# Two queues in place of one: the weight loads of a fused transformer kernel issued by ScalarE, the transfers through DRAM by SyncE

## The reference

```
first stack, per layer:
    z = rmsnorm(x) @ w_in            -> four kinds of attention, 4 heads each:
        block attention (rope), forget-gate attention, latent attention (up-projections), dilated mixture
    x += rmsnorm(concat(heads) @ w_out)
    x += rmsnorm((silu(h @ w_gate) * (h @ w_up)) @ w_down),   h = rmsnorm(x),  d_ff = 2816
second stack, per layer:
    x += 0.5 * rmsnorm(swiglu(rmsnorm(x)))                    d_ff = 2816
    b, c, v, p, gates = rmsnorm(x) @ w_in_2                   (width 6 * 1024)
    y = g_a * ((b * conv3(c * v)) @ w_conv_out) + g_p * (pool_mixer(p) @ w_pool_out)
    x += rmsnorm(y @ w_o)
    x += 0.5 * rmsnorm(swiglu(rmsnorm(x)))
```

## Time and profile before

| | us |
|---|---|
| three runs, median (lowest to highest) | 1735.21 (1733.9 to 1736.9) |
| the profiled execution, its own time | 1734.06 |
| its span, first to last instruction | 1732.3 |
| PE busy | 1720.9 (99%) |
| PEld busy | 1427.8 (82%) |
| DVE busy | 1232.8 (71%) |
| ACT busy | 924.6 (53%) |
| POOL busy | 117.6 (7%) |

### The profile page before, as it was taken

How to read it: one execution, slowest core, us unless ns; L and a number is a source line. 1 busy time by engine, 2 the same in 40 slices (tenths; PEclk the granted TensorE clock), 3 DMA queues, 4 the chain that set the end, 5 groups by cost and what they waited for, 6 DMA issues and landing times.

```text
span 1732.3 us, 22131 instructions
## 1 busy us (share of the span) xinstructions
PE 1720.9 (99%) x8077; PEld 1427.8 (82%) x8077; DVE 1232.8 (71%) x1581; ACT 924.6 (53%) x1438; POOL 117.6 (7%) x263
## 2 busy tenths in 40 slices
PE   9999999999999999999999999999999999999998
PEld 7888888888888888888888888888888888878887
DVE  8986656898655766666986866676656697686665
ACT  7665445767444554455564544465445556455443
POOL 5300000321000100000000100000000100010000
PEclk9999999999999999999999999999999999999999
DMA  8658776676777688768775777768786877568773
GB/s 269 196 179 255 231 231 196 189 227 209 234 230 227 215 242 255 236 206 278 231 254 204 223 242 230 228 213 254 243 253 198 268 236 251 205 201 256 232 221 122
DMA packets 351580, 392.84 MB, mean 227 GB/s; under 512 B 90512, under 2 KB 280496, under 8 KB 351216
## 3 DMA queue, kind: packets, MB, share of 16 engines
q1 hardware_dynamic: 348992, 383.68, 70.4%
q0 software_dynamic: 2176, 7.75, 1.4%
q10 hardware_dynamic: 304, 0.01, 0.0%
HBM read 357.82 MB, written 33.55 MB: 226 GB/s over the span
## 4 chain that ended last, share of the span: by engine, by line
PE 95%; DVE 2%; DMA 1%; POOL 1%; issue 0%; ACT 0%; DVEq 0%; SPq 0%; POOLq 0%; ACTq 0%
PE Dp L2407 28%; PE Gp L2407 19%; PE Tp L2407 19%; PE Dp L2375 8%; PE Dp L2376 8%; PE Dp L2377 8%; PE Dp L2427 2%; PE Gp L2615 1%; DVE wlo L1586 1%; PE Tp L2390 0%; DMA Z<-held_piece 0%; PE Dp L2646 0%; PE Tp L2646 0%; DMA stage<-held_piece 0%; DMA held_piece<-dil_masks 0%
## 5 line engine op out<-in xcount | busy, mean ns | idle before, releaser
L1586 DVE TENSOR_TENSOR wlo<-raw,whi 128x1024 fp32r<-128x1024 f32 (+1 forms) x608 | 716.9, 1215 | 259.5 <-ACT whi L1067 258.9
L1067 ACT ACTIVATE whi<-raw 128x1024 fp32r<-128x1024 f32 (+1 forms) x608 | 607.0, 1045 | 349.7 <-PE Dp L2407 96.4
L2407 PE MATMUL Dp<-whi,a_hi 128*128 128x512 f32 (+1 forms) x668 | 179.6, 390 | 0.4 <-DVE a_lo L1658 0.3
L2407 PE MATMUL Dp<-whi,a_lo 128*128 128x512 f32 (+1 forms) x668 | 178.0, 387 | 0.0
L2407 PE MATMUL Dp<-wlo,a_hi 128*128 128x512 f32 (+1 forms) x668 | 177.2, 387 | 0.0
L2407 PEld LDWEIGHTS Dp<-wlo,a_hi 128*128 128x128 f32 x668 | 124.8, 188 | 25.5 <-DVE wlo L1586 0.4
L2407 PEld LDWEIGHTS Dp<-whi,a_lo 128*128 128x128 f32 x668 | 124.6, 188 | 25.1
L2407 PEld LDWEIGHTS Dp<-whi,a_hi 128*128 128x128 f32 x668 | 122.7, 188 | 26.3 <-DVE a_lo L1658 1.5
L2375 PE MATMUL Dp<-whi,b_hi 128*128 128x512 f32 (+1 forms) x364 | 144.4, 397 | 0.0
L2377 PE MATMUL Dp<-whi,b_lo 128*128 128x512 f32 (+1 forms) x364 | 141.4, 389 | 0.0
L2376 PE MATMUL Dp<-wlo,b_hi 128*128 128x512 f32 (+1 forms) x364 | 141.4, 389 | 0.0
(11 more groups left out here) (298 smaller groups left out, 2223.8 us busy)
## 6 DMA issues: line engine op xcount, KB each, us to landing
raw<-in_ffn_w_gate_up SPq DMA_DIRECT2D x176, 512.0 KB, 5.0
raw<-in_w_in SPq DMA_DIRECT2D x132, 512.0 KB, 4.9
raw<-in_ffn_w_down SPq DMA_DIRECT2D x88, 512.0 KB, 4.4
raw<-in_w_gate SPq DMA_DIRECT2D x44, 512.0 KB, 4.0
raw<-in_w_up SPq DMA_DIRECT2D x44, 512.0 KB, 5.1
raw<-in_w_down SPq DMA_DIRECT2D x44, 512.0 KB, 4.4
held<-Z SPq DMA_DIRECT2D x132, 128.0 KB, 4.4
Z<-held SPq DMA_DIRECT2D x132, 128.0 KB, 4.7
```

The source lines that it names most:

```text
L1067: return nc.scalar.activation(whi[g % W][0:rows, c0:c0 + n], raw[g % R][0:rows, c0:c0 + n], ACT.Copy).then_inc(hi_done, 1)
L1586: return V.tensor_tensor(wlo[g % W][0:rows, c0:c0 + n], raw[g % R][0:rows, c0:c0 + n], whi[g % W][0:rows, c0:c0 + n].bitcast(F32), ALU.sub ...
L2407: return mm(bank, a[:, 4 * h + k, tile(t)], w[g % W][:, n * k:n * k + n], start=start, stop=stop, skip_group_check=True)
```

## The change

The list of what each unit loads is built ahead of all engines in a table `source`. SyncE issues units 0, 1 and 2 and from then on only what `behind(g)` issues. From unit 3 on ScalarE issues the weights: in `hi_b(g)`, so between the first and the second half of the cast of unit g, it waits for split_done of unit g-1 and issues the two DMAs of unit g+2.

```diff
-            def put(g, parts):
-                if g >= R:
-                    sp.wait_ge(split_done, 2 * (g - R) + 2)
-                if g == 0:
...
-                    return
-                for dst, src in parts:
-                    sp.dma_start(dst, src).then_inc(loaded[g % R], 16)
-                behind(g)
+            for g in range(LAST + 1):
+                first, second = source[g]
                 if g == 0:
+                    sp.dma_start(*first).then_inc(first_loaded, 16)
+                    sp.dma_start(*second).then_inc(loaded[0], 16)
                     x_half(1, 0)
                     x_half(0, 1)
                     x_half(1, 1)
+                elif g < R:
+                    sp.dma_start(*first).then_inc(loaded[g], 16)
+                    sp.dma_start(*second).then_inc(loaded[g], 16)
+                if g:
+                    behind(g)
...
+            def load(g):
+                act.wait_ge(split_done, 2 * (g - R) + 2)
+                first, second = source[g]
+                act.dma_start(*first).then_inc(loaded[g % R], 16)
+                act.dma_start(*second).then_inc(loaded[g % R], 16)
+
             def hi_b(g):
                 if g == 0:
                     act.wait_ge(loaded[0], 16)
+                elif g + R - 1 <= LAST:
+                    load(g + R - 1)
```

More of the change, by code:

```diff
@@ L583, in p_moved, with put, rows, half_rows @@
             return p_blocks[1].rearrange("p (q h e s) -> p h e q s", q=4, h=H, e=2)[:, h, e]
+        source = {}
+        def put(g, parts):
+            source[g] = parts
+        def rows(w):
+            return w.rearrange("l (k p) n -> l p k n", p=P)
+        def half_rows(g, w, l, h, c0, n):
+            r = raw[g % R][:, 0:4 * n].rearrange("p (k n) -> p k n", k=4)
+            put(g, [(r[:, 2 * e:2 * e + 2, :], w[l, :, 4 * h + 2 * e:4 * h + 2 * e + 2, c0:c0 + n])
+                    for e in range(2)])
@@ new lines, in all_rows, with two_rows, gate_up @@
+        def all_rows(g, w, l, c0):
+            r = raw[g % R][:, :].rearrange("p (k n) -> p k n", k=NK)
+            put(g, [(r[:, 4 * e:4 * e + 4, :], w[l, :, 4 * e:4 * e + 4, c0:c0 + 256]) for e in range(2)])
+        def two_rows(g, w, l, k0):
+            r = raw[g % R][:, :].rearrange("p (k n) -> p k n", k=2)
+            put(g, [(r[:, e:e + 1, :], w[l, :, k0 + e:k0 + e + 1, :]) for e in range(2)])
+        def gate_up(g, wg, wu, l, h, g0, u0):
+            r = raw[g % R][:, :].rearrange("p (k e n) -> p k e n", k=4, e=2)
+            put(g, [(r[:, :, 0, :], wg[l, :, 4 * h:4 * h + 4, g0:g0 + FC]),
+                    (r[:, :, 1, :], wu[l, :, 4 * h:4 * h + 4, u0:u0 + FC])])
@@ new lines, in build @@
+        w_in, w_out = rows(A["w_in"]), rows(A["w_out"])
+        w_g, w_u, w_d = rows(A["w_gate"]), rows(A["w_up"]), rows(A["w_down"])
+        q_up = A["w_mla_q_up"].rearrange("l (k p) n -> l p k n", p=QRH)
+        for l in range(LAYERS):
+            b = base1(l)
+            for h in range(2):
+                half_rows(b + LAT0 + h, w_in, l, h, C_LAT, LAT)
+            for h in range(2):
+                half_rows(b + MQ0 + h, w_in, l, h, C_MOBA, 512)
+            all_rows(b + MV, w_in, l, C_MOBA + 512)
+            for h in range(2):
+                half_rows(b + DQ0 + h, w_in, l, h, C_DIL, 512)
+            u = raw[(b + UPS) % R]
+            put(b + UPS, [(u[:, 0:512], A["w_mla_kv_up"][l]),
+                          (u[0:QRH, 512:1280].rearrange("p (k n) -> p k n", k=2), q_up[l])])
+            all_rows(b + DV, w_in, l, C_DIL + 512)
+            for h in range(2):
+                half_rows(b + FQ0 + h, w_in, l, h, C_FOX, 512)
+            all_rows(b + FV, w_in, l, C_FOX + 512)
+            for u, k0 in ((OUT_M, 0), (OUT_D, 6), (OUT_L, 4), (OUT_F, 2)):
+                two_rows(b + u, w_out, l, k0)
+            swiglu(b + FFN1, w_g, w_u, w_d, l, 0)
@@ new lines, in build, with project @@
+        w_in2, w_po, w_co, w_o = (rows(A[n]) for n in ("w_in_2", "w_pool_out_2", "w_conv_out_2", "w_o_2"))
+        gu1, gu2 = rows(A["ffn1_w_gate_up_2"]), rows(A["ffn2_w_gate_up_2"])
+        dn1, dn2 = rows(A["ffn1_w_down_2"]), rows(A["ffn2_w_down_2"])
+        wpg = A["w_pool_group_2"].rearrange("l g (k p) n -> l p g k n", p=P)
+        for l in range(LAYERS):
+            b = mixer2(l)
+            swiglu(base2(l), gu1, gu1, dn1, l, DFF)
+            def project(u, w, c0):
+                for c in range(2):
+                    for h in range(2):
+                        half_rows(b + u + 2 * c + h, w, l, h, c0 + 512 * c, 512)
+            project(0, w_in2, 3 * DM)
+            project(4, w_in2, DM)
+            project(8, w_in2, 2 * DM)
+            r = raw[(b + PG) % R][:, :].rearrange("p (g k n) -> p g k n", g=4, k=2)
+            put(b + PG, [(r[:, 2 * e:2 * e + 2, :, :], wpg[l, :, 2 * e:2 * e + 2, :, :]) for e in range(2)])
+            project(13, w_in2, 0)
+            project(17, w_in2, 4 * DM)
+            project(21, w_in2, 5 * DM)
+            project(25, w_po, 0)
+            project(29, w_co, 0)
+            for h in range(2):
+                for c in range(2):
+                    half_rows(b + 33 + 2 * h + c, w_o, l, h, 512 * c, 512)
+            swiglu(b + 37, gu2, gu2, dn2, l, DFF)
@@ L786, in all_rows @@
[L786 to L868, removed]
```

26 lines of the change are left out of this document (18 added, 8 removed).

## The result

| | before | after |
|---|---|---|
| time, us (median, lowest to highest) | 1734.7 (1733.9 to 1736.9) | 1749.45 (1747.49 to 1751.16) |
| ratio to before | | 1.0083 [1.0071, 1.0095] |
| span of the profiled execution, us | 1732.3 | 1747.7 |
| idle time of TensorE in it, us | 11.4 | 22.7 |

The changed kernel is 0.83% slower, 14.75 us by the medians. The forecast was slower by 4.5 us, 1739.7 us with a range up to 1747.5, so the direction came out and the size was off by a factor of three.

The account below looks back on a forecast made before the run. TensorE was taken as the bound, busy 1720.9 of 1732.3 us. Losses of 5.25 (first mixers) + 0.7 (stage ends) - 1.9 (last mixer) + 0.4 (first casts behind it) gave 4.45 us slower: 1739.7 us, range 1734.5 to 1747.5.

Parts of the forecast that it names:

- The steady state: In the FFNs, loads issued 2 us later still land in time and the pair costs zero to 0.1 us.
- Rival A: The pair is hidden behind the first half nowhere, 0.9 us more per tight cast: 11.7 us slower, 1747 us; chance 0.18.
- Places 1 and 3: First mixer at 28 to 32 us, first layer: 1.65 us lost; end of the first mixer, both layers: 1.5 us each.
- Place 2: Second layer's first mixer at 319 us: second half 1.85 us late, ScalarE's idle 0.86 us before line 1263; cost 1.0 us.
- The last mixer: End of the second layer's last mixer: the fetch flies nearly alone, so the 1.9 us wait for b_lo goes.
- Rival B: Transfers through DRAM get no faster, the 1.9 us stay, another 1.5 lost: 7.85 us slower, 1743 us; chance 0.14.
- Sum of the first mixers: Both layers' first mixers: 1.65 + 1.0 + 3.0 - 0.2 - 0.2 = 5.25 us lost.
- The lock that the forecast names: Issuing engines share a descriptor generator that each issue must lock; ScalarE's pair would at times wait, some tenths longer.
- Ends of stages: At the ten ends of stages together, 0.7 us for tenths not visible; the FFN ends were said to have slack.

Follow-up runs that it names:

- the first experiment: Changed kernel, but SyncE issues the weights cast in each layer's first mixer (units 2 to 19) in its old order: 1735.88 us, ratio 1.0006.
- the tail alone: Changed kernel, but ScalarE issues only units 36 to 39 of each second-stack mixer, SyncE all others as before: 1731.67 us, ratio 0.9984.
- the first mixers alone: Changed kernel, but ScalarE issues only units 2 to 19 of each layer's first mixer, SyncE all others in the old order: 1748.08 us, 1.0071.
- the two sets of units: Two variants of the changed kernel, ScalarE issuing only first-mixer units 13 to 16 (1739.9 us), or only units 2 to 12 and 17 to 19 (1740.52 us).

## Why the prediction was right in direction and wrong in size

**The steady state: right.** The pair is hidden behind the first half but for the few long issues, and the later load costs nothing. Rival A, which needs 0.9 us per tight cast, is refuted by 0.969 against 0.964 us in the median and by the first experiment. No cast of an FFN waits for raw.

**Places 1 and 3: right**, 1.63 for 1.65 and 1.64 for 1.5 each. The pair does come behind the wait with its whole length there (0.88 us from the first issue to the second half at place 1). With the pair moved behind the second half each costs 0.94 us less, since that half of the cast no longer waits, and the 0.7 left is the pair's.

**Place 2: too small**, 1.57 for 1.0. I read when the split ends from the trace of before, as if nothing ahead of it moved. But an earlier half in the same mixer is held back by its split in the same way, and VectorE behind it:

```profile
317.38 1.06 ACT L1072 ACTIVATE whi<-raw 128x1024 fp32r<-128x1024 f32 x1 [1.44 <-DVE wlo L1599]
318.99 0.69 DVE L1671 TENSOR_TENSOR a_lo<-stage,a_hi 128x512 fp32r<-128x512 f32 x1 [1.39 <-ACT a_hi L1145]
...
327.70 1.21 DVE L1599 TENSOR_TENSOR wlo<-raw,whi 128x1024 fp32r<-128x1024 f32 x1
```

The kernel is 7.06 us behind here, and the split that ended at 321.27 ends at 327.70 + 1.21 = 328.91, so 0.58 us later than I reckoned with; TensorE's first wait of the place (0.34 us, at 327.92) even begins before that. The pair took 1.07 us instead of 0.88. The slack of 0.86 us was there, but it takes less off a longer delay.

**The last mixer: right**, -2.05 for -1.9, by the mechanism given, and it is what makes the tail alone a gain (-2.8 us in the median, 2.4 between the profiled spans). Rival B (transfers no faster) is wrong here. Its general idea was nearer the truth elsewhere.

**The step that failed is "Sum of the first mixers", 5.25 us.** Measured, the first mixers lost 15.4 us: 6.5 at the places, 5.7 for blocks through DRAM and 3.2 at the lower clock. The sum priced only what ScalarE's queue holds back, and put the other two at nothing. I had seen for the last mixer that a load in front of a fetch makes the fetch slow, and that SyncE's order decides which comes first. I did not ask the same question in the first mixers, where the order of before was the good one: SyncE's waits for blocks kept the loads of units 13 to 16 behind the trips. With loads in another engine's queue this protection is gone. The experiments put 5.6 us on these eight units, and take 8.4 us away by making their loads small, a lower clock among them. The Trainium skill, DMA: Bandwidth & Descriptors, section Issuing engines are not separate DMA queues, says that DMAs of all issuing engines interleave on the same 16 DMA engines. The traces agree with it at this point (2.88 to 5.01 us for one fetch with a load beside it); I had used the sentence only as a rule against the gain, and it is as much a rule for the loss. The lock that the forecast names does not explain the long issues on SyncE in the changed kernel's trips, beside which ScalarE issued nothing.

**The clock: not in the sum.** It lost 3.2 us in the profiled execution. I argued that all waits together are 11.4 us and looked only at what new waits cost themselves. What decides whether the clock falls behind a wait stays open: with the same waits of 0.93 and 1.16 us at place 1 it fell in the changed kernel and not in the one with the first mixers alone.

**Ends of stages: 0.59 for 0.7**, but by luck at the seam of first mixer and FFN: I had put tenths there with no row behind them. SyncE's and ScalarE's rows there, changed kernel:

```profile
130.46 0.37 SPq L721 DMA_DIRECT2D stage<-held_x  x1
```

```profile
130.57 0.39 ACTq L1098 DMA_DIRECT2D raw<-in_w_gate  x1
```

The load goes out 0.1 us behind the fetch of x; it lands after 3.76 us and costs nothing. In three experiments the load went out first (its second DMA 0.3 to 1.35 us ahead), the fetch took 4.4 to 5.6 us, and TensorE lost 1.7 to 1.9 us in layer 0.

What isn't accounted for: 2 of the 13.8 us of the first mixers, which the two sets of units do not add up to. The 95% interval of the 13.8 alone is 2.7 us either way, so these 2 us may be noise.

## What to carry to other kernels

Moving DMAs to another engine's queue removes an order between transfers. List every small transfer on whose landing someone waits, see which bulk loads stood before and behind it in the old queue, and price both: here a tail gained 2 us and two mixers lost 5.7 us by the same mechanism. Move only those loads that stand ahead of a small transfer, and leave those that the old queue kept behind one. And where a change adds waits of a microsecond to the tightest engine, leave room for its clock: here another 3 us.

## What the runs showed of the hardware

- ScalarE issues DMAs while its datapath runs: an issue starts as little as 0.02 us after the start of the ACTIVATE ahead of it and takes 0.44 us in the median (0.33 to 1.45). The next ACTIVATE isn't late but for the few issues over 0.85 us (14 of 602). Such long ones are on SyncE's queue in the kernel before as well, 21 of about 1000, up to 2.3 us.
- The last of a block's fetches from DRAM (held_qk) took 2.7 to 2.9 us in the kernel before and in the five experiments in which SyncE holds the loads back, in both layers. In the changed kernel it took 5.0 and 6.7 us with a unit's load (two DMAs, together 1 MB) issued by ScalarE at its side. With a load's bytes cut to a sixteenth it took 3.5 and 3.6 us, now with no load beside it.
- The fetch of a half of x took 3.0 us with a load issued 0.4 us behind it from the same queue, 3.8 with one 0.1 us behind it from ScalarE's, and 4.4 to 5.6 with ScalarE's issued ahead of it (its second DMA by 0.3 to 1.35 us).
- Waits of TensorE of 1 to 2 us were followed in some executions by 3.4 us (once 6.8 us) at the lower clock, worth 1.6 to 1.7 us each time and 3 us for the long one. In others they were not.
